# Residual stream kept with features in partitions: norm by feature-tile sums and matmuls of ones, output weights stationary

## The reference, cut to what matters

```python
def trunk(x, mem, p):                       # run for two inputs: x (1, 512, 1024), mem (1, 256, 1024)
    for i in range(DEPTH):                  # DEPTH = 2, even: latent attention, odd: windowed attention
        h = rmsnorm(x, p['norm_in'][i])     # x * rsqrt(mean(x*x, features) + 1e-6) * gain
        z = h @ w_in                        # q, k, v parts, q_mem (512), gate (1536)
        mix = mla_mixer(...) if i % 2 == 0 else swa_mixer(...)
        mem_o = memory_attention(q_mem, mem, ...)   # kv = rmsnorm(mem) @ w_mem_kv, 4 heads of 128
        branch = jnp.concatenate([mix, mem_o], axis=-1) * jax.nn.silu(gate)
        x = x + branch @ p['w_out'][i]      # w_out (1536, 1024)
    return x
```

## Time and profile before

| | us |
|---|---|
| median of 3 runs | 1394.07 |
| lowest, highest | 1393.46, 1395.93 |
| the profiled execution | 1394.51 |
| its span (first to last instruction) | 1392.7 |
| TensorE matmuls busy | 1356.0 |
| DVE busy | 965.1 |
| ACT busy | 771.1 |
| POOL busy | 430.7 |

### The profile page before, as it was taken

One profiled execution on the slowest core, in us unless ns is written; L12 is line 12 of the kernel. 1 busy time (PEld: TensorE's weight loads), 2 busy tenths in 40 slices (PEclk: granted clock), 3 DMA queues, 4 the chain that ended last, 5 costly groups with the idle time before them and its releaser, 6 DMA issues.

```text
span 1392.7 us, 21120 instructions
## 1 busy us (share of the span) xinstructions
PE 1356.0 (97%) x7272; PEld 1174.2 (84%) x7272; DVE 965.1 (69%) x1979; ACT 771.1 (55%) x1791; POOL 430.7 (31%) x541
## 2 busy tenths in 40 slices
PE   6999999999999999999999999999999999999999
PEld 5889987888888889888888898888888888897887
DVE  6555688887664637888564656888876556489883
ACT  7344466555463537877463534665555444388771
POOL 2131243321121303766212213423302022238560
PEclk9999999999999999999999999999999999999999
DMA  6412221111442132322463132211123412233212
GB/s 215 133 50 81 77 89 56 40 61 45 142 150 65 54 98 80 109 61 78 151 195 93 51 91 78 78 57 50 39 92 108 130 56 76 75 94 96 69 50 99
DMA packets 81753, 122.39 MB, mean 88 GB/s; under 512 B 9584, under 2 KB 43760, under 8 KB 81648
## 3 DMA queue, kind: packets, MB, share of 16 engines
q1 hardware_dynamic: 76176, 113.35, 26.6%
q10 hardware_dynamic: 5472, 7.69, 1.8%
HBM read 116.82 MB, written 4.19 MB: 87 GB/s over the span
## 4 chain that ended last, share of the span: by engine, by line
PE 75%; DVE 8%; POOL 8%; ACT 5%; issue 3%; DMA 1%; SPq 0%; POOLq 0%; ACTq 0%; DVEq 0%
PE bank L1700 22%; PE bank L1702 22%; PE bank L1701 22%; PE bank L1745 5%; POOL rr L1515 3%; POOL prob L1575 3%; PE bank L1706 2%; PE bank L1707 1%; DVE w_lo_t L1033 1%; ACT prob L690 1%; DVE probT L1040 1%; PE bank L2041 1%; DVE part_lo L1033 1%; POOL qs_b L1670 1%; POOL rtmp L1514 1%
## 5 line engine op out<-in xcount | busy, mean ns | idle before, releaser
L1033 DVE TENSOR_TENSOR w_lo_t<-w_raw,w_hi 128x512 fp32r<-128x512 f32 (+3 forms) x436 | 257.2, 604 | 238.9 <-ACT w_hi L665 226.4
L665 ACT ACTIVATE w_hi<-w_raw 128x512 fp32r<-128x512 f32 (+3 forms) x440 | 227.9, 533 | 298.8 <-PE bank L1702 272.5
L1700 PE MATMUL bank<-w_hi,actT 128*128 128x512 f32 (+3 forms) x704 | 245.9, 349 | 1.8 <-DVE w_lo_t L1033 1.6
L1701 PE MATMUL bank<-w_lo_t,actT 128*128 128x512 f32 (+3 forms) x704 | 244.9, 348 | 0.0
L1575 POOL TENSOR_TENSOR prob<-prob,rinv 128x256 f32<-128x256 f32 x192 | 140.3, 761 | 236.2 <-DVE rinv L1138 236.2
L1702 PE MATMUL bank<-w_hi,actT 128*128 128x512 f32 (+3 forms) x512 | 170.1, 332 | 0.0
L1700 PE MATMUL bank<-actT,w_hi 128*128 128x512 f32 x384 | 152.5, 397 | 0.0
L1702 PE MATMUL bank<-actT,w_lo_t 128*128 128x512 f32 x384 | 150.0, 391 | 0.0
L1701 PE MATMUL bank<-actT,w_hi 128*128 128x512 f32 x384 | 149.9, 390 | 0.0
L1700 PEld LDWEIGHTS bank<-w_hi,actT 128*128 128x128 f32 x704 | 132.9, 189 | 17.9 <-DVE w_lo_t L1033 1.8
L1701 PEld LDWEIGHTS bank<-w_lo_t,actT 128*128 128x128 f32 x704 | 132.9, 189 | 14.7
(11 more groups left out here) (166 smaller groups left out, 3047.4 us busy)
## 6 DMA issues: line engine op xcount, KB each, us to landing
w_raw<-in_w_out SPq DMA_DIRECT2D x96, 256.0 KB, 2.7
w_raw<-in_w_mem SPq DMA_DIRECT2D x64, 256.0 KB, 2.7
w_raw<-in_w_b SPq DMA_DIRECT2D x112, 128.0 KB, 2.1
w_raw<-in_w_b SPq DMA_DIRECT2D x48, 256.0 KB, 2.7
w_raw<-in_w_a SPq DMA_DIRECT2D x32, 256.0 KB, 2.8
w_raw<-in_w_a SPq DMA_DIRECT2D x64, 128.0 KB, 2.1
bias<-in_alibi ACTq DMA_DIRECT2D x28, 192.0 KB, 2.4
w_raw<-in_w_qb SPq DMA_DIRECT2D x24, 192.0 KB, 2.4
```

Source lines behind the costliest of these rows:

```text
L665: act.activation(halves(n)[0], w_raw[:, n % RAW, 0:width], ACT.Copy).then_inc(w_hi_done, 1)
L1033: dve.tensor_tensor(halves(n)[1], w_raw[:, n % RAW, 0:width], halves(n)[0].bitcast(fp32), ALU.subtract).then_inc(w_lo_dve, 1)
L1700: nc.tensor.matmul(out, lhs[0], rhs[0], start=start, stop=False, skip_group_check=skip)
L1701: nc.tensor.matmul(out, lhs[0], rhs[1], start=False, stop=False, skip_group_check=skip)
```

## The change

x and y have their features in partitions in DRAM and in `xs`, so that x tile f is features 128f to 128f+127 of all 512 tokens. The 32 transposes of each layer, row_squares, row_norm and POOL's weight split go. In their place: ACT squares each feature tile (8 of 128x512), POOL adds the even ones and DVE the odd ones and the two sums. The sum is split in halves, and two matmuls of an all-ones stationary matrix give each token's sum in every partition (xsum). DVE picks the diagonal blocks and reduces them to one value for each partition and token tile, POOL takes the inverse root and multiplies it into a diagonal, that is split, and two more matmuls of ones (xR) give a 128x512 tile with each token's factor in every partition, which ACT copies to SBUF (`x_scale`). Then POOL multiplies each of the 8 x tiles by it into one of three slots, ACT writes the high half times the gain and DVE the low half, now from the slot. The queries wait for each feature tile alone, not for all. For odd L four squares, for L = 2 all eight, are made in the end of the layer before. In the output projection the weight columns are stationary and the branch halves move.

```diff
-                eng.dma_start(y[G, i * P:(i + 1) * P, c * CH:(c + 1) * CH],
-                              xs_of[:, G, i, c * CH:(c + 1) * CH]).then_inc(out_done, 16)
+                f = NT * c + i
+                eng.dma_start(y[G, f * P:(f + 1) * P, :], xs8[G][:, f, :]).then_inc(out_done, 16)
...
+                def x_square(L, f):
+
+                    if L % 2 == 0:
+                        act.wait_ge(x_in[f // 2], 16 * (L // 2 + 1))
+                    else:
+                        act.wait_ge(*read(("out", L - 1, f // NT, f % NT)))
+                    if f > 4:
+                        act.wait_ge(xsq_even if f % 2 == 1 else xsq_odd, 3 * L + (f - 3) // 2)
+                    out = (x_sq, x_sq_odd)[f] if f < 2 else x_slots[:, (f - 2) % 3, :]
+                    act.activation(out, xs8[L // 2][:, f, :], ACT.Square).then_inc(xsq_full, 1)
...
+                    elif l == 1:
+                        for f in range(NT, KD):
+                            x_square(L, f)
+                            if f % 2 == 1:
+                                w_hi_to(v_at + SPLIT + 1 + (f - NT) // 2)
+                    w_hi_to(v_at + SPLIT + 3)
+                    act.wait_ge(xsq_sum, L + 1)
+                    norm_hi(x_sq)
+                    w_hi_to(v_at + SPLIT + (8 if L == 0 else 7))
...
+                    w_hi_to(k_at + X_SCALE_AT + 2)
+                    act.wait_ge(diag_ready, L + 1)
+                    norm_hi(x_slots[:, 0, :])
+                    w_hi_to(k_at + X_SCALE_AT + 4)
+                    act.wait_ge(*full(("xR", L)))
+                    act.activation(x_scale, bank(("xR", L))[:], ACT.Copy).then_inc(read(("xR", L))[0], 1)
+                    w_hi_to(q_at + 1)
...
+                        act.wait_ge(x_scaled, KD * L + k + 1)
+                        a = GAIN_AT[f"in{l}"] + k
+                        act.activation(actT[:, k, :], x_slots[:, (k + 1) % 3, :], ACT.Copy, scale=gcol[:, a:a + 1]).then_inc(hi_done, 1)
+                        w_hi_to(q_at + min(k + 2, SPLIT + 2))
...
+                        for f in range(NT if l == 0 else KD):
+                            x_square(L + 1, f)
+                            w_hi_to(FIRST["out", L, 1, NT - 1] + SPLIT + f + 1)
...
+                def x_add(L, f):
+
+                    if f > 3:
+                        dve.wait_ge(xsq_odd, count.n["odd"])
+                    dve.wait_ge(xsq_full, KD * L + f + 1)
+                    dve.tensor_tensor(x_sq_odd, x_sq_odd, x_slots[:, (f - 2) % 3, :], ALU.add).then_inc(xsq_odd, 1)
+                    count("odd")
...
+                    use, v = ("xsum", L), x_slots[:, 2, :].rearrange("p (t n) -> p t n", t=NT)
+                    dve.wait_ge(*full(use))
+                    dve.tensor_tensor(v, bank(use)[:].rearrange("p (t n) -> p t n", t=NT),
+                                      ident[:].unsqueeze(1).to_broadcast([P, NT, P]), ALU.mult).then_inc(read(use)[0], 1)
+                    dve.wait_ge(*read(use))
+                    dve.reduce_sum(ss_x[:], v, AX).then_inc(ssx_ready, 1)
...
+                    elif l == 1:
+                        for f in (5, 7):
+                            w_lo_to(v_at + SPLIT + (f - NT) // 2)
+                            x_add(L, f)
+                    x_sum(L)
+                    w_lo_to(v_at + SPLIT + 3)
+                    norm_lo(x_sq)
+                    w_lo_to(v_at + SPLIT + (8 if L == 0 else 7))
+                    token_sums(L)
...
+                    w_lo_to(k_at + X_SCALE_AT + 2)
+                    norm_lo(x_slots[:, 0, :])
+                    w_lo_to(q_at + 1)
...
+                        dve.wait_ge(hi_done, count("hi"))
+                        dve.scalar_tensor_tensor(out=actT[:, KD + k, :], in0=x_slots[:, (k + 1) % 3, :], scalar=gcol[:, a:a + 1],
+                                                 in1=actT[:, k, :].bitcast(fp32), op0=ALU.mult,
+                                                 op1=ALU.subtract).then_inc(x_split, 1)
+                        w_lo_to(q_at + min(k + 2, SPLIT + 2))
                     norm([("memK", L, j) for j in range(NM)], MW, MH,
...
+                def x_norm(L):
+
+                    for f in (2, 4, 6):
+                        pool.wait_ge(xsq_full, KD * L + f + 1)
+                        if f > 2:
+                            pool.wait_ge(xsq_even, count.n["even"])
+                        pool.tensor_tensor(x_sq, x_sq, x_slots[:, (f - 2) % 3, :], ALU.add).then_inc(xsq_even, 1)
+                        count("even")
+                    pool.wait_ge(ssx_ready, L + 1)
+                    rsqrt(ss_x[:], rr_x[:], NT, D, rrx_ready)
+                    pool.wait_ge(rrx_ready, L + 1)
+                    pool.tensor_tensor(x_slots[:, 0, :].rearrange("p (t n) -> p t n", t=NT), ident[:].unsqueeze(1).to_broadcast([P, NT, P]),
+                                       rr_x[:].unsqueeze(2).to_broadcast([P, NT, P]), ALU.mult).then_inc(diag_ready, 1)
+                    pool.wait_ge(*read(("xR", L)))
+                    for k in range(KD):
+                        if k > 2:
+                            pool.wait_ge(x_split, KD * L + k - 2)
+                        pool.tensor_tensor(x_slots[:, (k + 1) % 3, :], xs8[L // 2][:, k, :], x_scale, ALU.mult).then_inc(x_scaled, 1)
...
-                                i = 2 * names[0][3] + b
-                                ins = mm3(bank(use)[:], (actT[:, k, i * P:(i + 1) * P], brlo[:, k, i * P:(i + 1) * P]), w, is_first, is_last)
+                                ins = mm3(bank(use)[:], cols(w, 2 * names[0][3] + b), (actT[:, k, :], brlo[:, k, :]), is_first, is_last)
...
+                    def across(use, n):
+
+                        pe.wait_ge(*vacant(use))
+                        pe.wait_ge(norm_split, n)
+                        for a in range(2):
+                            ins = nc.tensor.matmul(bank(use)[:], ones[:], norm_halves[:, a, :], start=a == 0, stop=a == 1)
+                        ins.then_inc(full(use)[0], 1)
...
+                    if L > 0:
+                        x_sums()
+                    mem_chunk("memK", {X_SCALE_AT: x_scales} if L > 0 else {0: x_sums, X_SCALE_AT: x_scales})
+
+                    def queries(k, j, w):
+                        if j == 0:
+                            pe.wait_ge(x_split, KD * L + k + 1)
+                        return hT(k, j), w
+
+                    project([("qmem", L, i) for i in range(NT)], KD, queries, lambda use: bank(use)[:, 0:MW])
...
-                            return (actT[:, ks[r], i * P:(i + 1) * P], brlo[:, ks[r], i * P:(i + 1) * P]), w
+                            return cols(w, i), (actT[:, ks[r], :], brlo[:, ks[r], :])
```

More of the change, by code:

```diff
@@ L196, in plan @@
             take([("memT", L, j) for j in range(KD // 2)])
-        chunk([("memV", L, j) for j in range(NM)], "mem", l, range(KD), MW, MW, MEM_LO)
-        take([("xT", L, k) for k in range(KD)])
+        chunk([("memV", L, j) for j in range(NM)], "mem", l, range(KD), MW, MW)
+        take([("xsum", L)])
         chunk([("memK", L, j) for j in range(NM)], "mem", l, range(KD), 0, MW)
+        take([("xR", L)])
         chunk(tokens("qmem", L), name, 0, range(KD), GATE0[l] - MW, MW)
@@ L770, in _ @@
                         act.wait_ge(ssm_ready, NM)
[L771 to L775, removed]
+                    v_at, k_at, q_at = (FIRST[n] for n in (("memV", L, NM - 1), ("memK", L, NM - 1), ("qmem", L, NT - 1)))
+                    if L == 0:
+                        w_hi_to(v_at + SPLIT + 2)
+                        for f in range(KD):
+                            x_square(L, f)
+                            if f % 2 == 1:
+                                w_hi_to(v_at + SPLIT + 3 + f // 2)
+                    elif l == 1:
+                        for f in range(NT, KD):
+                            x_square(L, f)
+                            if f % 2 == 1:
+                                w_hi_to(v_at + SPLIT + 1 + (f - NT) // 2)
[3 more added lines that the diff above has]
+                    w_hi_to(v_at + SPLIT + (8 if L == 0 else 7))
                     for j in range(NM):
@@ L1170, in _ @@
                 dve.memset(mhalf[:], -0.5).then_inc(mhalf_set, 1)
+                dve.memset(ones[:].bitcast(fp32), 1.0).then_inc(ones_set, 1)
                 for s in range(2):
@@ L1499, in _ @@
                             memory_columns(L + 1)
+                            for f in (3,) if l == 0 else (3, 5, 7):
+                                w_lo_to(FIRST["out", L, 1, NT - 1] + SPLIT + f)
+                                x_add(L + 1, f)
             @block.gpsimd
@@ L1539, in memory_scales @@
                     rsqrt(ss_m[:, at], rr_m[:, at], NM, D, rrm_ready)
-                def rows(tiles):
-                    for i in tiles:
-                        pool.wait_ge(ssx_ready, count("ssx"))
-                        rsqrt(ss_x[:, i:i + 1], rr_x[:, i:i + 1], 1, D, rrx_ready)
-                def w_lo(n):
-                    width = TILES[n][4]
```

(18 more changed lines are left out.)

95 lines of the change are left out of this document (43 added, 52 removed).

## The result

| | before | after |
|---|---|---|
| median of 5 runs (us) | 1394.77 | 1401.00 |
| lowest, highest | 1393.46, 1395.93 | 1399.88, 1401.22 |
| the profiled execution, its span | 1394.51, 1392.7 | 1401.0, 1399.2 |
| TensorE busy, DVE busy, POOL busy | 1356.0, 965.1, 430.7 | 1351.7, 1013.4, 482.1 |

The changed kernel is slower: the ratio to before is 1.0041, 95% interval [1.0031, 1.0052]. The forecast was 1400.0.

A forecast was written before the change was run, and what follows sets the result against it. TensorE, busy 97% of the span, was taken to bound the kernel. Removing 17.3 us, adding 3.6 of matmuls and waits of 3.4 + 4.4 x 2 + 7.4 gave +5.9, so 1400.0; its own range 1396 to 1404, overall 1385.5 to 1404.

The forecast's parts named there:

- What it removes and adds on TensorE: Layer starts: transposes and their waits go, 17.3 us; 16 matmuls of ones come, 3.6 us.
- 43.56 + 0.91: TensorE, per layer: 192 matmuls that stay, 43.56 us, and the added 4 matmuls of ones, 0.91.
- The output projection at nothing: Output projection: swapping the stationary side costs nothing; a turn 1% longer would cost 2.6 us.
- The turns at SBUF: Layer starts: POOL products, DVE low halves and splits take turns at one port, 2.30 to 2.36 us a round.
- The second rival: Query stretch: low half of x does not compete for the port, only splits and sums do; 1387.5, chance 0.14.
- The waits of a layer: TensorE's waits at layer starts: 3.4 us in L = 2, 4.4 in L = 1 and 3, 7.4 in L = 0.
- the forecast +5.9: Whole kernel: -17.3 + 3.6 + 3.4 + 4.4 x 2 + 7.4 = +5.9 us.
- Where inside a layer: Query rows: row 0 late by 0.73 us, row 1 by 0.65, row 6 by 1.74.
- work that does not wait: x and y transfers: same bytes in 4 and 2 KB runs, under work that does not wait, so no cost.
- The third rival: Layer starts: no turns at all, or all under slack; only L = 0's late weight stays; 1382.5, chance 0.09.

The follow-up runs named there:

- e5: e2 with POOL's three sums of squares a layer moved to DVE too; 1384.14 us, ratio 0.9927 to the kernel before.
- e4: Changed kernel with the branch stationary and the weights moving again in the output projection; 1401.32 us, ratio 1.0045 to the kernel before.
- e3: Changed kernel with the low half of x reading xR's PSUM bank, not the slot (wrong values), products still on POOL; 1387.89 us, ratio 0.9957.
- e2: Changed kernel with the 8 products a layer moved from POOL to DVE, reading the factor from PSUM, ACT's copy dropped; 1386.94 us, ratio 0.9945.
- e9: Changed kernel run again unaltered, beside e8 on the same chip; 1401.22 us, ratio 1.0047 to the kernel before.
- e8: Changed kernel with 4 more transposes in TensorE's pause ahead of the first value matmul; 1399.33 us, ratio 1.0031 to the kernel before.
- e7: e5 with 4 more transposes in TensorE's pause ahead of the first value matmul; 1385.62 us, ratio 0.9937 to the kernel before.

## Why the prediction was right

- **What it removes and adds on TensorE.** 17.3 out and 3.6 in were read from the order of time. After, the 196 matmuls of a layer without waits are 44.5 (e5), as 43.56 + 0.91 says. Right.
- **The output projection at nothing.** Right (e4).
- **The turns at SBUF.** Right in mechanism and size: low halves of 1.76 and products of 1.68 in a round of 2.30, forecast 2.30 to 2.36; the last low half is done 18.5 us after xR's turn (726.44 to 744.93), forecast 18.8. The Trainium skill, page "SBUF — State Buffer", section "Who interferes with whom", says that a DVE instruction with two SBUF inputs contends with a GpSimd instruction that reads SBUF, and one with at most one SBUF input does not (outside the 2-port modes). The traces agree for scalar_tensor_tensor: beside a product 1.76 with two SBUF inputs, and 0.74 in e3 with one in PSUM. For tensor_tensor the changed kernel's split of two SBUF inputs took 1.22 beside a product for 0.68; e2 can't add to this, since POOL multiplies no x tile there. The second rival, 1387.5, had bet against this.
- **The waits of a layer.** What was beyond the matmuls was forecast at 3.4, 4.4, 4.4 and 7.4 us for L = 2, 1, 3 and 0; measured 3.2, 4.1, 4.1 and 6.9 (53.63 - 44.47 - 2.3). The sum, -17.3 + 3.6 + 18.3, is +4.6 for the forecast +5.9. Even one by one the waits of L = 0 came close: 0.76 before key row 0, 1.38 before xsum, 0.88 before xR, 1.68 before the queries and 1.08 at row 6, for 0.9, 1.2, 0.8, 2.0 and 1.4.
- **Where inside a layer.** Right in L = 1 and 3: two late rows, 0.48 and 0.59 for 0.73 and 0.65, then row 6, 1.68 for 1.74. Partly wrong in L = 2. There row 0 waited 1.72 and not 0.73, row 1 not at all for 0.65, row 6 1.27 for 1.74. I let the split of query tile 0 take the port after POOL's first product. Its high half came only at 729.16 because the weight landed late, so three products went first. The load took 4.3 us (issued at 724.19), and 2.8 in L = 1 (401.42 to 404.20). In L = 2 alone the queue holds the first group's stores of y at that time, one between any two weight loads from 716.67 to 726.56; I had put them under work that does not wait. That they delay the load fits, and no run tests it. The low halves were late once instead of twice, and the total hardly moved.
- **What it missed.** The 2.3 us of the lower clock in L = 0, and 0.55 the other way for an earlier first matmul, which is partly chance: in e9, the same kernel, it came at 14.43 for 13.99. With the clock's part taken out by e8 (1399.3), the forecast of 1400.0 is 0.7 too high; with it, 1.0 too low. The measured time fits the forecast to 1.0 partly by luck, because these errors are of opposite sign: the layers' waits were forecast 1.3 too high, and the clock was not forecast at all.

The third rival, no turns at all, gave 1382.5. e5, which takes POOL out of the stretch, is at 1384.14: it was a good estimate of another kernel.

## What to carry to other kernels

Before handing work to the idle engine, ask what its neighbour reads at that moment: beside a POOL product of 1.29 us a DVE instruction with two SBUF inputs took 1.0 longer, and DVE alone did both jobs in less time. Keep one input in PSUM where it already is. And in a hand-written list, look at what stands behind the block that becomes late; here one weight split behind a norm made the largest waits (5.7 us over the four layers), and one number, changed on ACT and DVE, moved it.

## What the runs showed that was not expected

The page's clock row does not show the lower level at the start; only the distance of matmuls does (0.427 for 0.227), and it costs 2.3 us or nothing, by whether the clock rises before TensorE's pause of 0.7 to 1.1 us or only 3.4 to 5 us after it. Weights that land late in L = 3 held TensorE for 0.38 (e4), 0.74 (e3), 0.72 (e9), 0.99 (e8) and 1.24 us (e7) in profiles of kernels that had no such wait in others: for a difference under 1 us, one profile is not enough.
